# Gated one-hots of the expert gates made by ScalarE in fp32, later starts in the up stage, and first loads of the down stage issued earlier

## The reference

```python
q = (hf @ w_q).reshape(t, 8, 2, 128)
sc = einsum('thpc,hpnc->thpn', q, subkeys)
s1, i1 = top_k(sc[:, :, 0], 16);  s2, i2 = top_k(sc[:, :, 1], 16)
top_s, top_p = top_k(s1[..., None] + s2[..., None, :], 16)      # of 256 pairs
e1, e2 = i1[top_p // 16], i2[top_p % 16]                         # expert e1*128 + e2
gates = softmax(top_s)                                           # 8 heads x 16 = 128 a token
act = gelu(x . u[expert]) * gates
y = sum(act * v[expert])
```

## Time and profile before

| | us |
|---|---|
| median of 3 runs | 2923.48 (2920.71 to 2927.77) |
| profiled execution, own time | 2923.21 |
| its span, first to last instruction | 2921.1 |
| TensorE busy | 2730.2 (93%) |
| VectorE busy | 2395.6 (82%) |
| GpSimd busy | 1384.3 (47%) |
| ScalarE busy | 1270.7 (44%) |
| mean granted TensorE clock | 0.966 of full |

### The profile page before, as it was taken

The page is one execution under the profiler, slowest core; times in us unless marked ns, Lnnn a source line. Parts: engine busy times, 40 slices in busy tenths (PEclk is TensorE's granted clock), DMA queues, the critical chain, the costliest instruction groups (busy, mean ns, idle before and its releaser), DMA issues. The chain is left out here.

```text
span 2921.1 us, 40294 instructions
## 1 busy us (share of the span) xinstructions
PE 2730.2 (93%) x15003; PEld 2392.9 (82%) x15003; DVE 2395.6 (82%) x4253; ACT 1270.7 (44%) x2539; POOL 1384.3 (47%) x909
## 2 busy tenths in 40 slices
PE   7999699989989996999999999995999999999996
PEld 6777466449989996999999999994888888888885
DVE  3284787238988889999999999984999999999987
ACT  4244333113322232888888888862222222222222
POOL 1011210004326674656666666652566666666663
PEclk9999799989999998999999999997999999999998
DMA  4110100323217776999999999998999999999996
GB/s 120 36 40 18 58 1 1 94 72 98 69 59 245 245 244 243 369 381 388 372 386 353 399 365 388 394 386 291 362 369 375 379 375 376 388 376 373 378 368 211
DMA packets 332099, 762.67 MB, mean 261 GB/s; under 512 B 23216, under 2 KB 158384, under 8 KB 329344
## 3 DMA queue, kind: packets, MB, share of 16 engines
q0 software_dynamic: 111104, 403.02, 37.1%
q1 hardware_dynamic: 219872, 353.41, 34.2%
q10 hardware_dynamic: 928, 3.67, 0.3%
HBM read 667.73 MB, written 92.27 MB: 260 GB/s over the span
## 5 line engine op out<-in xcount | busy, mean ns | idle before, releaser
L1552 PE MATMUL expert_pre<-h2T,uT_hi 128*128 128x320 f32 x4096 | 674.5, 313 | 56.7 <-DVE uT_lo L1741 46.6
L1867 POOL DMA_INDIRECT v_rows<-in_peer_v,row_numbers x336 | 542.2, 1614 | 372.2 <-DVE y_rest L1932 221.7
L1650 POOL DMA_INDIRECT u_rows<-in_peer_u,row_numbers x384 | 536.2, 1396 | 312.5 <-DVE row_weights L1671 258.9
L1552 PEld LDWEIGHTS expert_pre<-h2T,uT_hi 128*128 128x128 f32 x4096 | 615.9, 190 | 63.3 <-DVE uT_lo L1741 53.2
L1671 DVE CUSTOM_DVE_ANT_0 u_rows<-u_rows,h_rows_kept 128x1024 f32<-128x1024 f32 x384 | 478.7, 1265 | 73.5 <-DMA u_rows<-in_peer_u,row_numbers 73.1
L1966 PE MATMUL expert_out<-v_hi,w_hi 128*128 128x512 f32 x1280 | 500.7, 391 | 34.8 <-DVE y_rest L1924 19.6
L1966 PE MATMUL expert_out<-v_lo,w_hi 128*128 128x512 f32 x1280 | 499.8, 390 | 0.0
L1966 PE MATMUL expert_out<-v_hi,w_lo 128*128 128x512 f32 x1280 | 499.5, 390 | 0.0
L1932 DVE SCALAR_TENSOR_TENSOR y_rest<-v_rows,row_weights,y_rest 128x1024 f32<-128x1024 f32 x256 | 327.4, 1280 | 25.3 <-DMA v_rows<-in_peer_v,row_numbers 24.6
L1552 PE MATMUL expert_pre<-h2T,uT_lo 128*128 128x320 f32 x2048 | 343.3, 309 | 0.0
L1552 PEld LDWEIGHTS expert_pre<-h2T,uT_lo 128*128 128x128 f32 x2048 | 313.0, 189 | 0.0
(11 more groups left out here) (317 smaller groups left out, 4455.3 us busy)
## 6 DMA issues: line engine op xcount, KB each, us to landing
u_chunk<-in_peer_u_turned SPq DMA_DIRECT2D x128, 512.0 KB, 7.7
pick_memory<-in_peer_v SPq DMA_DIRECT2D x128, 512.0 KB, 9.4
acts_dram<-expert_acts SPq DMA_DIRECT2D x128, 320.0 KB, 5.5
gates_dram<-pick_memory SPq DMA_DIRECT2D x20, 2048.0 KB, 11.1
pick_memory<-acts_dram SPq DMA_DIRECT2D x128, 320.0 KB, 10.3
pick_memory<-gates_dram SPq DMA_DIRECT2D x32, 1280.0 KB, 17.8
wq_tile<-in_peer_wq SPq DMA_DIRECT2D x32, 512.0 KB, 4.0
w_in_columns<-in_w_in SPq DMA_DIRECT2D x20, 512.0 KB, 4.0
```

The lines of the kernel that those rows point to most:

```text
L1552: last = nc.tensor.matmul(pre[:, (2 * c + half) % 4, 0:WIDTH], part[:, c % 2, k], m.h2T[:, t, k, HALVES[half]], start=n == 0, stop=n == le ...
L1650: pool.indirect_dma_start(rows[:, k % RING], None, table, bass.IndirectOffsetOnAxis(ap=m.row_of[:, f, slot:slot + 1], axis=0)).then_inc(fe ...
L1867: pool.indirect_dma_start(rows[:, k % ROW_RING], None, d.peer_v, bass.IndirectOffsetOnAxis(ap=m.row_of[:, f, slot:slot + 1], axis=0)).then ...
```

## The change

- The second one-hot is made by ScalarE alone, in fp32. `distance` writes |key number - e2| for each of 128 places (Abs, with minus e2 as a bias column); `gate` turns it into relu(gate - gate x distance), which is the gate at e2 and zero at every other key (Relu, with minus the gate as scale and the gate as bias column). `keep` makes both negated columns in one operation. VectorE makes the first one-hot alone.
- Both operands of the spread product are fp32 and not split, so one product stands for two.
- Low halves: GpSimd makes those of chunks under 42, of all even chunks, and of the last four; VectorE the odd ones from 43 to 123.
- Key parts start at quarter 128, spreading runs from 160 to 500, rows after the early ones from 140 to 508.
- The first three loads of the down stage and the first gates are issued after the store of chunk 126 and not 127. Later gates are loaded two chunks ahead, so the second gates load belongs to these first loads too.

```diff
@@ -1421,8 +1421,8 @@
     QUARTERS = 4 * NK
-    POOL_LOWS = 32
-    KEYS_FROM, SPREAD_FROM, SPREAD_TO = 120, 144, QUARTERS - 16
+    by_pool = lambda c: c < 42 or c % 2 == 0 or c >= NK - 4
+    KEYS_FROM, SPREAD_FROM, SPREAD_TO = 128, 160, QUARTERS - 12
     EARLY_DOTS, ROWS_TO = 48, QUARTERS - 4
@@ -1434,7 +1434,7 @@
     rows_by = lambda q: (EARLY_DOTS * q // KEYS_FROM if q < KEYS_FROM else
-                         EARLY_DOTS + paced(q, ROWS - EARLY_DOTS, KEYS_FROM, ROWS_TO))
+                         EARLY_DOTS + paced(q, ROWS - EARLY_DOTS, KEYS_FROM + 12, ROWS_TO))
     rows_at = lambda q: range(rows_by(q), rows_by(q + 1))
@@ -1459,9 +1459,8 @@
         act_out = sb("expert_acts", [P, 2, DENSE])
-        first_hot = sb("first_hot", [P, SLOTS, GROUP, NK], F32R)
-        second_hi = sb("second_hot_hi", [P, SLOTS, GROUP, NK], F32R)
-        second_lo = sb("second_hot_lo", [P, SLOTS, GROUP, NK], F32R)
+        first_hot = sb("first_hot", [P, SLOTS, GROUP, NK])
+        second = sb("gated_second_hot", [P, SLOTS, GROUP, NK])
         spread = m.pick_memory[:, 0:2 * NK * 32].rearrange("p (b e t) -> p b e t", b=2, t=32)
@@ -1469,7 +1468,7 @@
         routeT = sb("routeT", [P, 2, 3, P])
-        gate_hi, gate_lo = sb("gateT_hi", [P, 2, P], F32R), sb("gateT_lo", [P, 2, P])
+        minus = sb("minus_second_and_gate", [P, 2, 2, P])
         rows = sb("u_rows", [P, RING, D])
@@ -1483,7 +1482,7 @@
         act_stored, y_first_in = m.act_stored, sem("y_first_in")
-        hot_done, gates_hot = sem("hot_done"), sem("gates_hot")
+        hot_done, apart_done, gates_hot = sem("hot_done"), sem("second_apart"), sem("gates_hot")
         spread_done, spread_read = sem("spread_done"), sem("spread_read")
@@ -1497,10 +1496,10 @@
 
-            if c < POOL_LOWS:
-                engine.wait_ge(ulo_pool, c + 1)
+            if by_pool(c):
+                engine.wait_ge(ulo_pool, sum(1 for b in range(c + 1) if by_pool(b)))
             else:
-                engine.wait_ge(ulo_dve, c - POOL_LOWS + 1)
+                engine.wait_ge(ulo_dve, sum(1 for b in range(c + 1) if not by_pool(b)))
 
@@ -1527,22 +1526,22 @@
                         sp.dma_start(m.y_first[:], d.x2[0:P, :]).then_inc(y_first_in, 16)
-                for b in range(2):
-                    sp.wait_ge(spread_stored[b], 16 * (ALL // PART // 2))
-                for x in range(DOWN_LOADS):
-                    load_down(sp, d, m, x)
-
+                    if c == NK - 2:
+                        for b in range(2):
+                            sp.wait_ge(spread_stored[b], 16 * (ALL // PART // 2))
+                        load_gates(sp, d, m, 0)
+                        for x in range(DOWN_LOADS):
+                            load_down(sp, d, m, x)
             @block.tensor
...
                 def spread_out(g):
+                    pe.wait_ge(hot_done, g + 1)
                     pe.wait_ge(gates_hot, g + 1)
...
                     for j in range(GROUP):
-                        nc.tensor.matmul(spread_ps[:, g % 2, j], first_hot[:, g % SLOTS, j],
-                                         second_hi[:, g % SLOTS, j], start=True, stop=False)
                         last = nc.tensor.matmul(spread_ps[:, g % 2, j], first_hot[:, g % SLOTS, j],
-                                                second_lo[:, g % SLOTS, j], start=False, stop=True)
+                                                second[:, g % SLOTS, j], start=True, stop=True)
                     last.then_inc(spread_done, 1)
@@ -1557,7 +1556,7 @@
                     if dense_nth[t]:
-                        pe.wait_ge(routeT_done, 3 * dense_nth[t])
+                        pe.wait_ge(routeT_done, 2 * dense_nth[t])
                     for n in range(3):
@@ -1603,15 +1602,24 @@
                 high(0)
+                def distance(g):
+                    i, first = g // GROUPS, g % GROUPS * GROUP
+                    if first == 0:
+                        act.wait_ge(routeT_done, 2 * i + 2)
+                    if g >= SLOTS:
+                        act.wait_ge(spread_done, g - SLOTS + 1)
+                    for j in range(GROUP):
+                        last = A(second[:, g % SLOTS, j], m.iota[:], ACT.Abs,
+                                 bias=minus[:, i % 2, 0, first + j:first + j + 1])
+                    last.then_inc(apart_done, 1)
+
                 def gate(g):
-                    t, first = g // GROUPS, g % GROUPS * GROUP
-                    act.wait_ge(hot_done, g + 1)
+                    i, first = g // GROUPS, g % GROUPS * GROUP
+                    act.wait_ge(apart_done, g + 1)
                     for j in range(GROUP):
-                        A(second_lo[:, g % SLOTS, j], second_hi[:, g % SLOTS, j].bitcast(F32), ACT.Identity,
-                          scale=gate_lo[:, t % 2, first + j:first + j + 1])
-                    for j in range(GROUP):
-                        last = A(second_hi[:, g % SLOTS, j], second_hi[:, g % SLOTS, j].bitcast(F32), ACT.Identity,
-                                 scale=gate_hi[:, t % 2, first + j:first + j + 1].bitcast(F32))
+                        last = A(second[:, g % SLOTS, j], second[:, g % SLOTS, j], ACT.Relu,
+                                 scale=minus[:, i % 2, 1, first + j:first + j + 1],
+                                 bias=routeT[:, i % 2, 2, first + j:first + j + 1])
                     last.then_inc(gates_hot, 1)
@@ -1622,6 +1630,8 @@
                         spread_out(g)
+                    for g in hots_at(q):
+                        distance(g)
                     for g in gates_at(q):
@@ -1653,7 +1663,7 @@
                     c = q // 4
-                    if q % 4 == 1 and c + 1 < POOL_LOWS:
+                    if q % 4 == 1 and c + 1 < NK and by_pool(c + 1):
                         low(c + 1)
@@ -1728,13 +1738,10 @@
                         v.tensor_copy(routeT[:, i % 2], route_ps[:]).then_inc(routeT_done, 1)
-                    elif n == 1:
-                        dve.wait_ge(routeT_done, 3 * i + 1)
-                        v.tensor_copy(gate_hi[:, i % 2], routeT[:, i % 2, 2]).then_inc(routeT_done, 1)
                     else:
-                        dve.wait_ge(routeT_done, 3 * i + 2)
-                        v.tensor_tensor(gate_lo[:, i % 2], routeT[:, i % 2, 2], gate_hi[:, i % 2].bitcast(F32),
-                                        ALU.subtract).then_inc(routeT_done, 1)
+                        dve.wait_ge(routeT_done, 2 * i + 1)
+                        v.tensor_scalar(minus[:, i % 2], routeT[:, i % 2, 1:3], -1.0, None, ALU.mult
+                                        ).then_inc(routeT_done, 1)
 
@@ -1745,23 +1752,22 @@
                     if first == 0:
-                        dve.wait_ge(routeT_done, 3 * i + 3)
+                        dve.wait_ge(routeT_done, 2 * i + 1)
                     if g >= SLOTS:
                         dve.wait_ge(spread_done, g - SLOTS + 1)
-                    v.tensor_tensor(first_hot[:, g % SLOTS], keys, each(routeT[:, i % 2, 0, tokens]), ALU.is_equal)
-                    v.tensor_tensor(second_hi[:, g % SLOTS], keys, each(routeT[:, i % 2, 1, tokens]), ALU.is_equal
+                    v.tensor_tensor(first_hot[:, g % SLOTS], keys, each(routeT[:, i % 2, 0, tokens]), ALU.is_equal
                                     ).then_inc(hot_done, 1)
...
                     c = q // 4
-                    if q % 4 == 1 and POOL_LOWS <= c + 1 < NK:
+                    if q % 4 == 1 and c + 1 < NK and not by_pool(c + 1):
                         low(c + 1)
...
                             key(t, n)
-                    for n in range(3):
+                    for n in range(2):
                         for t in tiles_at(q, TURN_AFTER + 2 + n):
@@ -1787,6 +1793,13 @@
 
+def load_gates(sp, d, m, n):
+    if n >= 2:
+        sp.wait_ge(m.prod_done, DOWN_C * (n - 1))
+    sp.dma_start(m.gate[:, n % 2], d.gates[:, :, DOWN_C * n:DOWN_C * n + DOWN_C, :].rearrange("t p c k -> p t c k")
+                 ).then_inc(m.g_in[n % 2], 16)
+
@@ -1802,11 +1815,8 @@
     sp.dma_start(m.prod[:, x % W_RING], d.acts[x]).then_inc(m.a_in[x % W_RING], 16)
-    if c == 0:
-        if n >= 2:
-            sp.wait_ge(m.prod_done, DOWN_C * (n - 1))
-        sp.dma_start(m.gate[:, n % 2], d.gates[:, :, DOWN_C * n:DOWN_C * n + DOWN_C, :].rearrange("t p c k -> p t c k")
-                     ).then_inc(m.g_in[n % 2], 16)
+    if c == DOWN_C - 2 and n + 1 < d.NK // DOWN_C:
+        load_gates(sp, d, m, n + 1)
```

## The result

The changed kernel takes 2955.07 us (median; 2953.62 to 2967.06), the kernel before 2923.37 beside it: ratio 1.0116, 95% interval 1.0093 to 1.0139. It is slower, by about 1%. The profiled execution has a span of 2952.7 us, 31.6 more than before.

The account below looks back on a forecast made before the run. It took VectorE, whose low halves TensorE waits for, to bound the spread stage (790 us against 754 needed). Gains of 27 (up stage) and 12 (transition) off the 2921.1 span gave 2882, plus 2.1: 2884 us, range 2852 to 2922.

Parts of the forecast that it names:

- Part 4: VectorE and GpSimd in the spread stage: a GpSimd low half costs VectorE 2.3 us; stage 770 us, between 748 and 806.
- its last term: VectorE's waiting for gathered rows in the spread stage, through the ring of six: 32 us or more.
- The same loss: Spread stage: no engine has room, so it loses 36 us as before, against TensorE's need of 735, giving 770.
- second rival: Spread stage: the ring of rows binds, a row still takes 2.27 us, stage 806; 2931 us, slower; chance 0.13.
- Part 1: Low halves of chunks 32 to 41 on GpSimd: TensorE loses 6 us, reaching quarter 160 at 1166.
- Part 2: Spread product: one fp32 product for two fp32r takes 0.83 us a group against 0.84; TensorE neither gains nor loses.
- Part 3: ScalarE's one-hots: a second column adds 92 ns, Relu 480 ns, 59 us more; its stage work becomes 734 us.
- Part 5: Last chunks of the up stage: u load ahead of the last store; twelve quarters take 21.1 + 1.5 us.
- Part 6: First down loads, issued at chunk 126, 7 us earlier: 12 of the transition's 58.7 us gained.
- third rival: Transition: last store held behind the second gates load, engines pass 5 us later than before; 2901 us; chance 0.14.
- first rival: Engines fit together well: spread stage at TensorE's pace, 748 us; gain 73, giving 2850 us; chance 0.18.
- The fourth: Rival on ScalarE: Abs or Relu not in the gelu's table, loads of 1283 ns add over 400 us; 3300; chance 0.02.

Follow-up runs that it names:

- p4: The changed kernel, but VectorE makes all low halves from chunk 42 on: 2900.74 us, ratio 0.9940.
- p2: The kernel before with only ScalarE's fp32 one-hots and the single fp32 product added: 2893.43 us, ratio 0.9917.
- q2: p4 with GpSimd also filling an unused 128x2560 tile with zeros at 45 places: 2940.57 us, ratio 1.0051.
- r1: p4 with the 48 early rows gathered at the pace of the kernel before (due by quarter 120): 2891.57 us, ratio 0.9913.
- p3: The kernel before with only the earlier first loads of the down stage and gates two chunks ahead: 2910.98 us, ratio 0.9976.
- q4: The kernel before with the changes of p2 and p3 together, start times and low halves as before: 2886.79 us, ratio 0.9865.
- r3: q4 with the second gates load issued behind the last store of activations: 2886.52 us, ratio 0.9894.

## Why the prediction was wrong

Forecast 2884 us, faster; measured 2955.07, outside the range of 2852 to 2922.

**Part 4 failed, in its last term.** Its price of a low half was right. Dots, one-hots and added rows grew by 317 x 0.208 + 158 x 0.109 + 39 x 0.278 = 94 us (first one-hot 792 ns against 683), for 44 low halves: 2.1 each, forecast 2.3. VectorE's busy time was 701, forecast 693. What was mis-sized is the waiting for rows: "32 or more" was taken, which is the value of before, and 100 us were measured. With it VectorE's list is not 725 but 701 + 100 + 18 (for ScalarE's high parts, taken at nothing) = 819, the length of the stage.

Two things were left out of that term. The wait of before was the wait of a VectorE full of work: take work away, and the rows come no sooner, so part of the time saved turns into waiting. p4, in which GpSimd makes at most one low half in the stage, already waits 87 us for rows, p2 (none) 66. There it costs little, since VectorE's work is only 652 to 656 us. And GpSimd's absence: the turn of a place was worked out as 1.6 to 1.85 us a row, with the landing at its median (8.4 before, 8.5 after) and each gather issued at once. In fact an operation of 2.3 us at 45 places adds 35 us of waiting for rows (p4 to q2), and in after the gathers behind a low half follow each other only every 1.4 + 0.3 us. The longer waits and the held operations meet on one engine, and fill it.

"The same loss" of 36 us was a guess with no mechanism behind it. The loss became 817 - 735 = 82: about 50 of TensorE's idle time and some 33 of matmuls slower than their best pace (17 before), at a mean granted clock of 0.97 and not 1.00. TensorE's timeline shows how the second follows the first:

```profile
1172.14 2.62 PE L1551 MATMUL expert_pre<-h2T,uT_hi 128*128 128x320 f32 x16 [1.78 <-POOL uT_lo L1649]
1182.97 3.66 PE L1551 MATMUL expert_pre<-h2T,uT_hi 128*128 128x320 f32 x16 [3.52 <-POOL uT_lo L1649]
```

The same sixteen matmuls take 2.62 us behind a wait of 1.78 and 3.66 behind one of 3.52; the mean granted clock was 1.00 in 1172.1 to 1174.6 and 0.68 in 1182.97 to 1186.4, between the levels of 1.2 and 2.4 GHz.

**The second rival came true in the main**: GpSimd's low half stands in the ring of six, and a seventh place takes 35 us off. It was given 0.13. Its number for a row proves nothing by itself: 817.1/355 = 2.30 us is the length of the stage, whatever sets it. And its premise, that a row still takes 2.27 us, does not hold: p4 brings the same rows through the same ring in 2.1 to 2.2 us each. The argument against it, that GpSimd idled 229 us waiting for VectorE and not for a transfer, decides nothing: GpSimd waits for VectorE when VectorE is slow and also when the ring is short, 175 us in the fast p4 and 107 in after. Its price was low by 24 us: 817 for its 806, 79 for its 71, and the transition.

**Part 1 failed in a term that was not in it.** Quarter 160 came at 1182.97, forecast 1166, and that with the 4.4 us that this profile had gained ahead of the stage. The waits for low halves were 0.84 + 1.30 + 1.78 + 3.52 = 7.4 us, forecast 6. "VectorE's key parts start at 1110.65 as before" was wrong: the first stood at 1123.76, and TensorE waited 16.6 us for the route. VectorE's 48th early dot ended at 1094.6 and not 1085.2, since `EARLY_DOTS * q // KEYS_FROM` stretches with KEYS_FROM (r1: 10.8 us), and the decoding behind it took 3.7 us more, low halves falling on it.

**Part 2 was right.** TensorE's timeline in the spreading:

```profile
1515.85 1.05 PE L1543 MATMUL spread_ps<-gated_second_hot,first_hot 128*128 128x128 f32 x8
1516.66 0.83 PE L1551 MATMUL expert_pre<-h2T,uT_hi 128*128 128x320 f32 x4
```

Eight records for four products, and the next matmul starts 0.81 us after the first, forecast 0.83. As VectorE loses a one-hot of 681 ns a group, the fp32 form alone gains 25 us (p2).

**Part 3 was right.** Relu with two columns takes 482 ns, forecast 480; ScalarE's stage sum 717, forecast 734.

**Part 5 was right**: 23.7 us, forecast 22.6, and the 4.68 of the earlier trace rows is gone.

**Part 6 was half right**: 6.8 us gained (8 in p3), forecast 12. The hold fell on the last store, as the third rival had it, and the second gates load was no longer waited for. SyncE's and ScalarE's timelines:

```profile
2025.49 8.22 SPq L1518 DMA_DIRECT2D acts_dram<-expert_acts  x1
```
```profile
2035.07 1.06 ACT L1899 ACTIVATE v_hi<-pick_memory 128x1024 fp32r<-128x1024 f32 x1 [10.73 <-PEq L1504]
```

The first rival fell with the stage. Its 13 us of slow matmuls were misread besides: TensorE's idle time in that stage is 789.6 - 771.4 = 18.2 us and not 23, which makes them 17 and the rival's stage 752. The fourth fell too: the gelu's line has two table loads in the whole execution, as before, and abs and relu have none.

## What to carry to other kernels

Where two engines pass buffers round a ring, an operation put into the issuing engine's list costs by how long it keeps that engine from issuing, even if it touches nothing else. Waits of both sides of a ring for each other do not yet say that the ring is the bound: p4, q4 and after all show them, and only in after did the stage hang on them. Ask whether the waiting engine has time to wait: add up its work and its waits, see which of them the change moves, and do not carry a wait over from a kernel in which the engine had more to do. One more place is the cheap test, and was here the cheap cure (35 us). When a start time moves, look for every pace that is divided by it.

## What was not expected of the hardware

An operation of VectorE with one input was held as well. VectorE's timeline of after, while GpSimd makes low halves:

```profile
1101.97 2.69 DVE L1191 TENSOR_SCALAR pick_memory<-pick_memory 128x640 f32<-128x640 f32 x1
...
1106.17 0.48 DVE L1191 TENSOR_SCALAR pick_memory<-pick_memory 128x640 f32<-128x640 f32 x1
```

2.69 us against 0.48 for the same operation; the slow one begins 0.11 us after a low half of GpSimd has begun (1101.86, 2.45 us long) and ends 0.35 us after its end. The Trainium skill has this in "SBUF — State Buffer", Who interferes with whom: tensor_scalar can enter a mode that takes the pair of ports shared with GpSimd. The forecast had counted only operations with two operands.

SyncE was held at the first issue behind a load of gates in the transition: 2.87 and 8.22 us in after, 5.25 and 15.96 and 7.25 in before, 3.96 and 18.9 in r3, where issues that do not follow such a load take 0.3 to 1.0. An order of loads on that queue is also an order of holds. What sets their length was not tested.
